# Scattering each group's results at its own end, in a one-core decoder layer with a mixture of experts

## The reference, cut to what matters

```
h = (_rms(x, norm1_g) * (1.0 + sc1) + sh1)
z = h @ w_in
...
y = jnp.concatenate([y_m, y_b, y_r, y_n], axis=-1) @ w_out
x = x + g1 * y
h2 = (_rms(x, norm2_g) * (1.0 + sc2) + sh2)
lg, le = h2 @ wg + bg, h2 @ we + be
...
_, grp = lax.top_k(lg, 1)
top_p, top_i = lax.top_k(jax.nn.softmax(le_g, axis=-1), TOP_K_IN_GROUP)
...
y_e = (jax.nn.silu(xblk @ w1[e]) * (xblk @ w3[e])) @ w2[e]
return x + g2 * hier_moe(...)
```

## Time and profile before

| | us |
|---|---|
| timed runs, median of 3 | 1609.42 (1607.70 to 1611.62) |
| the profiled execution | 1606.35 |
| its span in the trace | 1604.5 |
| PE busy | 1335.1 (83%) |
| DVE busy | 666.7 (42%) |
| moved by the DMA engines | 609.83 MB, mean 380 GB/s |

### The profile page before, as it was taken

How to read it: one execution, slowest core, us unless ns; L and a number is a source line. 1 busy time by engine, 2 the same in 40 slices (tenths; PEclk the granted TensorE clock), 3 DMA queues, 4 the chain that set the end, 5 groups by cost and what they waited for, 6 DMA issues and landing times.

```text
span 1604.5 us, 18063 instructions
## 1 busy us (share of the span) xinstructions
PE 1335.1 (83%) x7501; PEld 804.9 (50%) x7501; DVE 666.7 (42%) x852; ACT 202.5 (13%) x502; POOL 28.7 (2%) x32
## 2 busy tenths in 40 slices
PE   6999999999999989989667677678767767767867
PEld 5767888888988858744123123223223213223223
DVE  5768686887676777241121121121122112112212
ACT  3001222221132111211001001001001001001001
POOL 0000000000010000100000000000000000000000
PEclk9999999999999999999788888887788888787879
DMA  9999687856875796999999999999999999999997
GB/s 394 426 425 383 254 328 301 329 220 253 320 307 220 313 374 272 391 405 424 428 428 428 429 428 428 429 428 428 428 429 429 428 428 429 429 428 429 428 429 294
DMA packets 45257, 609.83 MB, mean 380 GB/s; under 512 B 4976, under 2 KB 5504, under 8 KB 6944
## 3 DMA queue, kind: packets, MB, share of 16 engines
q1 hardware_dynamic: 44000, 604.26, 90.1%
q0 software_dynamic: 784, 4.34, 0.7%
q10 hardware_dynamic: 432, 0.65, 0.1%
HBM read 607.13 MB, written 2.10 MB: 380 GB/s over the span
## 4 chain that ended last, share of the span: by engine, by line
DMA 53%; PE 41%; DVE 3%; ACT 1%; issue 1%; SPq 0%; POOL 0%; ACTq 0%; DVEq 0%; POOLq 0%
DMA ring<-in_exp_w 35%; PE W L684 19%; DMA Zpad<-in_exp_w 9%; DMA ring<-in_stream 6%; PE M L1102 5%; PE W L661 3%; DMA tail<-in_exp_w 3%; PE W L985 2%; PE A L1120 2%; PE W L1054 2%; DVE ring L1467 1%; PE W L1067 1%; PE W L638 1%; PE W L1011 1%; PE M L1074 1%
## 5 line engine op out<-in xcount | busy, mean ns | idle before, releaser
L1102 PE MATMUL M<-ring,g1b 128*32 128x512 f32 x1280 | 183.4, 704 | 76.7 <-DMA ring<-in_exp_w 76.5
L1467 DVE CUSTOM_DVE_ANT_0 ring<-ring,tail 128x2048 f32<-128x2048 f32 x96 | 221.3, 2349 | 47.1 <-DMA ring<-in_stream 47.1
L1413 DVE TENSOR_TENSOR consts<-A,tail 32x512 f32<-32x512 f32 x128 | 87.8, 686 | 159.9 <-PE A L1120 156.9
L2011 DVE SCALAR_TENSOR_TENSOR tail<-tail,M 128x128 f32<-128x128 f32 x32 | 9.2, 288 | 299.3 <-ACT tail L1390 299.3
L1102 PEld LDWEIGHTS M<-ring,g1b 128*32 128x32 f32 x1280 | 38.9, 119 | 186.3 <-DMA ring<-in_exp_w 113.5
L684 PE MATMUL W<-ring,buf_x 128*128 128x256 f32 x576 | 128.9, 380 | 0.5 <-DVE ring L1413 0.5
L684 PE MATMUL W<-ring,buf_h 128*128 128x256 f32 x576 | 128.7, 380 | 0.0
L684 PEld LDWEIGHTS W<-ring,buf_x 128*128 128x128 f32 x576 | 108.4, 190 | 16.4 <-DVE ring L1413 0.9
L684 PEld LDWEIGHTS W<-ring,buf_h 128*128 128x128 f32 x576 | 108.6, 190 | 15.4 <-issue 1.1
L1074 PEld LDWEIGHTS M<-consts,tail 128*128 128x128 f32 x512 | 66.6, 203 | 93.2 <-ACT tail L1392 60.3
L1120 PE MATMUL A<-Zpad,tail 128*32 128x512 f32 x512 | 85.1, 795 | 29.3 <-DMA Zpad<-in_exp_w 22.5
(11 more groups left out here) (331 smaller groups left out, 1403.8 us busy)
## 6 DMA issues: line engine op xcount, KB each, us to landing
ring<-in_exp_w SPq DMA_DIRECT2D x96, 2048.0 KB, 36.6
ring<-in_stream SPq DMA_DIRECT2D x86, 2048.0 KB, 13.0
Zpad<-in_exp_w SPq DMA_DIRECT2D x56, 2048.0 KB, 38.0
PPY<-in_exp_w SPq DMA_DIRECT2D x24, 2048.0 KB, 30.6
tail<-in_exp_w SPq DMA_DIRECT2D x16, 2048.0 KB, 45.4
Zpad<-in_early SPq DMA_DIRECT2D x16, 1024.0 KB, 19.5
buf_x<-in_x SPq DMA_DIRECT2D x2, 1024.0 KB, 6.3
buf_h<-in_x POOLq DMA_DIRECT2D x1, 2048.0 KB, 19.7
```

The costliest lines, as they stand in the source:

```text
L1102: ins = pe.matmul(M[32 * j:32 * j + 32, 512 * w13:512 * w13 + 512], XT[:, kk, 32 * q:32 * q + 32], w[:, 512 * k:512 * k + 512], start=(kk ...
L1413: return dve.tensor_tensor(o, x, y, op)
L1467: ins = dve.tensor_tensor_reduce(w, w, c_rows[:], 1.0, first[:, j:j + 1], ALU.mult, ALU.add, to[:, j:j + 1])
```

## The change

- The fetch of x waits until the second weight half of block 1 has landed.
- DVE makes the sums for block 1's products 2 and 3 ahead of block 0's residual, which now multiplies in PSUM; ACT copies block 1's first four corners ahead of the squares.
- Block 3's weights are stored by columns: each half holds all rows of 256 columns.
- The diagonals for the gate g2 are formed between the two last residuals.
- The two best experts are found by ranks: for every pair of the 8 experts one comparison, summed.
- `gather` runs in halves; the first expert of a group uses w1 and w3 for the first half of the width, then the second half is gathered. The gates are worked out behind the first half.
- Each group is scattered at the end of its own q = 3, block by block into `W`, `M` and `A`; the part behind the loop is gone. POOL's fill of `ysb` shrinks to 128 columns.

```diff
+                if (q, part) in ((0, 0), (0, 1)):
+                    part, hf = hf, part
                 place, full, _ = expert_ring[SLOT_OF[j]]
...
                 elif j == 9:
-                    sp.wait_ge(sem["g2_ready"], 1)
+                    sp.wait_ge(sem["x1_squared"], 5)
+                    sp.wait_ge(sem["g2_summed"], 1)
...
-                elif (step, arg) == ('chunk', CHUNKS[-1]):
-
-                    item_done(pool, 'chunk', arg)
-                    pool.dma_start(x1, a['x'][0].rearrange("(a p) d -> p a d", p=P)).then_inc(sem["x_again"], 16)
+            item_done(pool, 'chunk', CHUNKS[-1])
+            i = STREAM.index(('wout', 1, 1))
+            pool.wait_ge(slot_full[i % RING], 16 * (i // RING + 1))
+            pool.dma_start(x1, a['x'][0].rearrange("(a p) d -> p a d", p=P)).then_inc(sem["x_again"], 16)
...
-                pool.memset(ysb[32 * q:32 * q + 32, :], 0.0).then_inc(sem["y_copied"], 4)
-                pool.wait_ge(sem["y_copied"], 4 * q + 4)
+            pool.memset(ysb[:, 0:64], 0.0).then_inc(sem["y_copied"], 16)
+            pool.memset(ysb[:, 64:128], 0.0).then_inc(sem["y_added"], 8)
 
...
-                    w0 = half_arrives()
-                    half[0] += 1
-                    w1 = half_arrives()
-                    half[0] += 1
                     for c in range(2):
+                        w = half_arrives()
                         for kk in range(KT):
-                            w = w0 if kk < 8 else w1
                             for tt in range(TT):
                                 p0 = o + 512 * c + 256 * tt
-                                p1 = 512 * (kk % 8) + 256 * c
-                                ins = pe.matmul(W[:, p0:p0 + 256], YT[:, kk, tt * P:tt * P + P], w[:, p1:p1 + 256],
+                                ins = pe.matmul(W[:, p0:p0 + 256], YT[:, kk, tt * P:tt * P + P],
+                                                w[:, 256 * kk:256 * kk + 256],
                                                 start=(kk == 0 and tt == 0), stop=(kk == KT - 1), skip_group_check=True)
+                        half_done(ins)
...
-            def gather():
-
-                for b in range(4):
+            def gather(hf):
+
+                for b in range(2 * hf, 2 * hf + 2):
                     for k in range(4 * b, 4 * b + 4):
                         for tt in range(TT):
...
 
             def scatter(n):
 
-                pe.wait_ge(sem["gt_ready"], n + 1)
-                pe.wait_ge(sem["y_copied"], 16 * n + 16)
-                for tt in range(TT):
-
-                    if tt == 1:
-                        pe.wait_ge(sem["y_added"], 2 * n + 1)
-                    for b in range(4):
-                        ins = pe.matmul(W[:, 512 * b:512 * b + 512], GT[:, tt * P:tt * P + P],
-                                        ysb[:, 512 * b:512 * b + 512], start=True, stop=True)
-                    ins.then_inc(sem["scattered"], 1)
+                pe.wait_ge(sem["gt_ready"], n + 2)
+                pe.wait_ge(sem["xt_act"], 2 * n + 3)
+                pe.wait_ge(sem["xt_dve"], 2 * n + 3)
+                for b in range(4):
+                    pe.wait_ge(sem["y_copied"], 16 * n + (29 + b))
+                    pe.matmul(W[:, 512 * b:512 * b + 512], GT[:, 0:P], ysb[:, 512 * b:512 * b + 512],
+                              start=True, stop=True).then_inc(sem["scattered"], 1)
+                    pe.matmul(M[:, 512 * b:512 * b + 512] if b < 3 else A[:], GT[:, P:2 * P],
+                              ysb[:, 512 * b:512 * b + 512], start=True, stop=True).then_inc(sem["scattered"], 1)
...
-                                        pe.wait_ge(sem["gt_ready"], it + 2)
-                                    pe.wait_ge(sem["part_copied"], 8 * it + (2 * q + 1))
-                                    sum_and_turn(h1T).then_inc(sem["h_turned"], 1)
+                            pe.wait_ge(sem["y_added"], 8 * it + 8)
+                            gather(0)
+                        for i in range(4):
+                            w13, hf = (i % 2, i // 2) if q == 0 else (i // 2, i % 2)
+                            if (q, i) in ((0, 0), (0, 1)):
+                                pe.wait_ge(sem["y_added"], 8 * it + (2 * i + 2))
+                            if (q, i) == (0, 2):
+                                pe.wait_ge(sem["y_added"], 8 * it + 8)
+                                pe.wait_ge(sem["g2_ready"], 2)
+                                gather(1)
+                            if q == 0 and w13 == 0:
+                                pe.wait_ge(sem["xt_act"], 2 * it + (hf + 1))
+                                pe.wait_ge(sem["xt_dve"], 2 * it + (hf + 1))
+                            w = expert_arrives(pe, it, 6 * q + i)
+                            for k in range(8):
+                                kk = 8 * hf + k
+                                j = k % 4
+                                ins = pe.matmul(M[32 * j:32 * j + 32, 512 * w13:512 * w13 + 512],
+                                                XT[:, kk, 32 * q:32 * q + 32], w[:, 512 * k:512 * k + 512],
...
-                        if q == 0:
-
+                        if q == 3:
                             scatter(it)
...
-                if i == 0 and name[:3] == 'out':
-                    act.wait_ge(sem["x1_ready"], int(name[3:]))
+                if (name, i) == ('out2', 0):
+                    act.wait_ge(sem["x1_ready"], 2)
...
+            for i in range(4):
+                copy_corner('out1', i)
             square_sums(0, slice(0, 512))
-            for i in range(5):
-                copy_corner('out1', i)
+            copy_corner('out1', 4)
...
             act.wait_ge(sem["g2_summed"], 1)
             for m in range(4):
                 ins = act.activation(g2c[32 * m:32 * m + 32, :], W[32 * m:32 * m + 32, 512 * m:512 * m + 512], ACT.Copy)
-            ins.then_inc(sem["g2_ready"], 1)
+                if m % 2 == 1:
+                    ins.then_inc(sem["g2_ready"], 1)
+            def dress_tokens(n, hf):
+
+                act.wait_ge(sem["gathered"], 4 * n + (2 * hf + 1))
+                for k in range(8 * hf, 8 * hf + 4):
+                    ins = act.activation(XT[:, k, :], W[:, k * P:k * P + P], ACT.Identity,
+                                         scale=gsc[:, KT + k:KT + k + 1],
+                                         bias=modc[:, 3 * KT + k:3 * KT + k + 1])
+                ins.then_inc(sem["xt_act"], 1)
...
                     dve.wait_ge(sem["g1_copied"], 4)
                 width = d.stop - d.start
-                t3 = tmp[:, 0:TT * width].rearrange("p (a d) -> p a d", a=TT)
-                tt_op(t3, w_ap.rearrange("p (a d) -> p a d", a=TT), g1b[:, d].unsqueeze(1).to_broadcast([P, TT, width]),
+                w3 = w_ap.rearrange("p (a d) -> p a d", a=TT)
+                t3 = w3 if n == 0 else tmp[:, 0:TT * width].rearrange("p (a d) -> p a d", a=TT)
+                tt_op(t3, w3, g1b[:, d].unsqueeze(1).to_broadcast([P, TT, width]),
                       ALU.mult).then_inc(sem["dve_step"], 1)
                 dve.wait_ge(sem["dve_step"], step_no())
                 tt_op(x1[:, :, d], x1[:, :, d], t3, ALU.add).then_inc(sem["x1_ready"], 1)
...
             token_sums('out1')
             sums_31('out1')
             for n in range(3):
-                if n == 0:
-                    item_done(dve, 'wout', n)
-                    residual(n, W[:, 1024:2048], slice(0, 512))
-                else:
+                if n > 0:
                     corners(f'out{n}')
                     residual(n, tmp[:, 0:1024], slice(512 * n, 512 * n + 512))
                 if n < 2:
                     sums_24(f'out{n + 1}')
                 if n == 0:
+                    item_done(dve, 'wout', n)
+                    residual(n, W[:, 1024:2048], slice(0, 512))
                     scale_router()
                     ada_accumulate(*ADA_BEHIND[1][0])
                     sums_31('out2')
...
             dve.tensor_scalar(jdesc, const('iota'), -1.0, 33.0, ALU.mult, ALU.add)
-            dve.wait_ge(sem["wout_part"], 1)
+            places = const('iota')[:, 0:EPG]
+            tt_op(ahead, places.unsqueeze(1).to_broadcast([P, EPG, EPG]), places.unsqueeze(2).to_broadcast([P, EPG, EPG]),
+                  ALU.is_lt).then_inc(sem["dve_step"], 1)
+            dve.wait_ge(sem["dve_step"], step_no())
+            dve.wait_ge(half_used, halves_used(STREAM.index(('wout', 3, 0)) + 1)[0])
             residual(3, W[:, 0:512], slice(1536, 1792))
+            dve.wait_ge(sem["ada_half_used"], halves_used(EXPERT_BASE)[1])
+            diagonals(g2_diag, g2_cols).then_inc(sem["diag_ready"], 1)
             item_done(dve, 'wout', 3)
             residual(4, W[:, 512:1024], slice(1792, 2048))
-            dve.wait_ge(sem["ada_half_used"], halves_used(EXPERT_BASE)[1])
-            diagonals(g2_diag, g2_cols).then_inc(sem["diag_ready"], 1)
...
```

(29 more changed lines are left out.)

127 lines of the change are left out of this document (53 added, 74 removed).

## The result

The changed kernel takes 1596.39 us (median of 4 executions, 1595.12 to 1597.12), the kernel before 1610.07 (1607.70 to 1611.62): ratio 0.9927, interval 0.9913 to 0.9940. That is 13.7 us faster, and outside the range 1598.5 to 1608 that was forecast. Timed again in five rounds the two medians are 1596.81 and 1608.55 (ratio 0.9923, 0.9909 to 0.9937), 11.7 us apart. The two profiles differ by 11.2 us of span, 1604.5 and 1593.3, and these are what the sum was about: 6.0 was forecast.

A forecast was written before the change was run, and what follows sets the result against it. The prediction took the expert phase as bound by bytes, its end hanging on PE finishing half 0. Terms 2.8 - 1.7 + 0.3 + 1.1 + 2.0 + 1.5 = 6.0 us gave 1603.4 us, range 1598.5 to 1608.

The forecast's parts named there:

- What bounds the kernel: Expert phase: bound by bytes at 428 GB/s; each microsecond PE finishes half 0 sooner takes one off the end.
- the landing of block 1's weights: First output blocks: without x's 2.10 MB beside them, 5.0 us at 420 GB/s, the weights land near 580.9 instead of 585.93.
- 10.46 us to product 2: Block 2, from its sums to product 2: sums, corners and residual 8.12 us, then the sum for product 2, 2.34.
- Gain 2.8: Block 2's product 2 starts at 619.5 instead of 622.29, with x landing at 597; 1.1 with x at its bound.
- charge of 1.7 for the clock: Ahead of block 2's product 2: PE idles from 615.3 to 619.5, and the products behind it cost 1.7 us more.
- Block 3: 0.3 forecast: Block 3 by columns starts with its first half, saving 0.3 us; the earlier issue of half 6 by itself frees nothing.
- Diagonals and ranks: Router ahead of half 0: diagonals off the path, about 0.3 us counting, and a shorter ranking; together 1.1 us.
- Gather: 2.0 + 1.5 forecast: Gather to half 0: 32 matmuls instead of 64 gain 2.0 us; keeping the higher clock gains 1.5.
- The second gather and the groups' ends: Between halves 1 and 2 and at group ends: halves 10 and 11 and the ring cover the delays; no loss.
- The scatter "gains nothing": Next group's first expert: removing the scatter that stood inside it gains nothing, as this phase is bound by bytes.
- Rival (c): Expert loads from 628 on: engines never idle again, gain 8.5 to 9.9 us; chance 0.71 together with the forecast.
- Rival (b): Blocks 0 to 2: x lands too late, holding DVE's residual and block 2's product 2; 1609 to 1615 us, chance 0.07.

The follow-up runs named there:

- x_too_late: The changed kernel, but POOL issues x only when block 2's first weight half has landed instead of block 1's second; 1611.6 us, ratio 1.001 to the kernel before.
- split_first: The changed kernel with PE's wait for DVE's tokens moved to a half's fifth product and two expert halves issued ahead of block 3's weights; 1596.15 us, ratio 0.9922.
- split_first_warm: split_first with 7.7 us of products for nothing at each group's fourth expert; 1597.08 us, ratio 0.9930 to the kernel before.

## Why the forecast fell short, step by step

- **What bounds the kernel: right.** From half 10's issue to the last half it is 894.9 to 895.5 us in the first profiles of both kernels and in twelve of the runs, whose half 10 came between 99 and 117 us behind block 1's first product; a delay ahead of half 0 comes back one to one. In two runs it is 895.8 and 896.1, and in four 897.2 to 899.3: there the loads had a gap behind or just ahead of half 10, or the DMA engines ended unevenly.
- **The step that failed is the landing of block 1's weights** ("Its 2.10 MB are 5.0 us at 420 GB/s; without it the weights land near 580.9"). They landed at 576.6, 9.2 us sooner and not 5. The forecast took x's bytes out of this stretch and nothing else. But 0.5 MB of router loads had left it too, which POOL's order in the change shows and the forecast did not cost, and in the kernel before the engines moved well under 428 GB/s while POOL's last small load was on its way (to 578.3) and once more behind it, some 2 us that no byte count shows:

```profile
574.00:576.00 2.00, 2.00 (x6) 0.87 (x5) 2.00 (x3) 0.00 (x0) 0.00 (x0) 1.00 1.13 200
576.00:578.00 2.00, 2.00 (x6) 0.95 (x5) 2.00 (x3) 0.00 (x0) 0.00 (x0) 1.00 0.90 369
...
582.00:584.00 2.00, 2.00 (x8) 1.33 (x7) 0.66 (x1) 0.00 (x0) 0.00 (x0) 1.00 0.63 262
```

  The runs bear out that these loads make it: with x alone put back the weights land 6.3 us later, with x and the router's loads at their old place 9.3. How the part beyond x's bytes divides between the router's bytes and the slower engines is read from these rows; no run separates them. From that landing the errors follow: x was issued at 577.2 and not 581.0, met idle engines and landed in 7.9 us (585.1 and not 597), so that next to nothing of it stood ahead of block 2's weights, whose sums began at 605.56 and not 609. From there on the forecast's 10.46 us to product 2 are exact (616.02). The term "Gain 2.8" measured 6.1.
- **The charge of 1.7 for the clock** was not due: the idle time ahead of block 2's product 2 was 0.94 and not 4.2. The price was right: in x_too_late 4.04 us of idle time at this very place cost 1.7. It was charged where the idle time no longer was.
- **Block 3: 0.3 forecast, 0.42 measured,** but it also keeps 2.0 us that the earlier half 10 would have lost to a gap in the loads. The reason given for its being worth nothing failed.
- **Diagonals and ranks: 1.1 forecast, 1.3 measured;** the diagonals 0.2 to 0.3 of it. No run undid the ranks: their part is read from the places.
- **Gather: 2.0 + 1.5 forecast, 3.45 measured** from its start to half 0. The 1.5 is in part luck: it holds against the first profile of the kernel before, whose gather took 9.01 us. Against the second one, 7.38 us behind the same idle stretches, the gain is 1.8 and nothing of it is clock. So the reason given, that the idle stretches ahead of the old gather cost it its clock, is not shown. No run undid the halved gather either.
- **The second gather and the groups' ends** cost nothing, as forecast: half 12 is issued at 691.63, 9.05 behind half 10, and from 690 to 696 the loads show no gap (the 0.7 us at 684 are lost ahead of half 10's data).
- **The scatter "gains nothing"** holds for seven groups of eight. In the first one there is no backlog behind it; in the second profile of the kernel before, it and the lower clock around it cost 4 us there. That this is the source of its wider spread (1604.6 to 1612.4, against 1594.6 to 1597.9) is read from two profiles and was not tried by itself.
- **Rival (c)** had the right frame: its 8.5 us came from halves that run without a gap from block 3 on, and they do; block 3's are issued at 623.04, and the engines are busy again from 624 on instead of 628.
- **Rival (b)** has its chain and price shown (x_too_late) and its case absent: x landed in 7.9 us while DVE did two-input sums from 576.68 to 581.4. The engines moved 422 GB/s from 580 to 582, and had x stood still until 581.4, its 2.10 MB would have had to come at over 570 GB/s, where full engines move some 430 here. The Trainium skill ("SBUF — State Buffer", section "Who interferes with whom") describes a hold of loads of the GpSimd queue by certain DVE operations and infers that operations with two tensors as inputs do not hold them. The trace agrees.

The change's 11.3 us are thus: 6.1 from loads and DVE's order at blocks 1 and 2 (2.8 undone alone, 1.6 undone alone, 5.2 together), 0.4 block 3, 1.3 ranks and diagonals, 3.45 gather, of which 1.6 is the clock that the old gather had in one execution.

## What to carry to other kernels

Where a phase is bound by bytes to its end, find the one issue that starts it and count everything from there; then a microsecond is worth one ahead of it, and nothing behind it as long as the loads have no gap. Here the loads that were moved out of a busy stretch gave back more time than their bytes, and x landed sooner for it; forecast both landings again from the new issue, not from the old duration. Two edits that cure the same idle time can hide a part of each other when only one is undone (0.8 of 5.2 us here), so undo them together as well, and at the exact place. And take a second profile of the kernel before: one execution can have a clock in a place that the next one does not.

## What the runs showed of the hardware that was not expected

- A 2048 KB load of POOL's queue took 7.9 us on idle engines and 18.8 to 19.7 beside loads of SP's queue. From 553 to 561 us of the kernel before the engines moved 2.38 MB of SP's and 1.05 MB of POOL's queue. The Trainium skill ("DMA: Bandwidth & Descriptors", section "Queues, rings and completion order") says that each engine takes the queues that have work in turn, a packet at a time. The trace agrees: the load takes its share at once (31% here) instead of queueing behind the others.
- PE's idle time costs more than itself, but not always: behind 3.2 and 3.3 us of it the two products of block 1 took 7.17 us (granted clock 1.00), behind 4.34, 5.27 and 5.37 us 8.81, 8.80 and 9.70 (0.50 for a part). Nor is the idle time all of it: behind the same short idle stretches the old gather took 9.01 us in one execution and 7.38 in another.
- The last half takes between 1.92 and 3.64 us by the clock that PE has there, which differs between executions of one kernel (3.23 and 2.44 in the kernel before) and between kernels that differ hundreds of microseconds earlier. It is as large as most of the edits here, and hides them in the time.
- The DMA engines do not end together: the share at the end fades within 2 us in the changed kernel and over 4 us in two others (split_first and split_first_warm), and PE starts the last half only when it is down to 0.
